# Layer 0's input projection moved up beside the context path, and its cross-attention keys computed inside its own attention

## What is computed

```python
def even_mixer(x, positions, w_in, sinks, sgu_ln_g, sgu_ln_b, sgu_w, sgu_b, w_out):
    h = x @ w_in                                   # 1024 -> 1792: q 512, k 128, v 128, bu 512, bv 512
    ...
    q = partial_rope(q.reshape(bsz, s_len, A_Q_HEADS, HEAD_DIM), positions)
    k = partial_rope(k.reshape(bsz, s_len, A_KV_HEADS, HEAD_DIM), positions)
    a_out = sliding_window_sink_attention(q, k, v, sinks)
    b_out = chunked_spatial_gating(jax.nn.gelu(bu), jax.nn.gelu(bv), sgu_ln_g, sgu_ln_b, sgu_w, sgu_b)
    return jnp.concatenate([a_out, b_out], axis=-1) @ w_out
...
        x = layer_norm(ALPHA * x + mix, ln1_g, ln1_b)
        x = layer_norm(ALPHA * x + memory_cross_attention(x, mem, xq, xkv, xo), ln2_g, ln2_b)
        x = layer_norm(ALPHA * x + grouped_moe(x, router_w, router_bias, e_gate, e_up, e_down), ln3_g, ln3_b)
```

## Time and profile before

| | |
|---|---|
| median of 3 runs | 2438.23 us (2437.54 to 2438.71) |
| profiled execution | 2439.04 us |
| its span | 2437.2 us |
| granted TensorE clock, mean | 0.91 of 2.4 GHz |
| PE busy | 1992.4 us, 82% |
| POOL busy | 1001.4 us, 41% |
| DVE busy, ACT busy | 737.3 us, 734.9 us, 30% each |
| HBM traffic | 479.5 MB, 197 GB/s over the span |

### The profile page before, as it was taken

One profiled execution on the slowest core, in us unless ns is written; L12 is line 12 of the kernel. 1 busy time (PEld: TensorE's weight loads), 2 busy tenths in 40 slices (PEclk: granted clock), 3 DMA queues, 4 the chain that ended last, 5 costly groups with the idle time before them and its releaser, 6 DMA issues. The chain is left out here.

```text
span 2437.2 us, 29352 instructions
## 1 busy us (share of the span) xinstructions
PE 1992.4 (82%) x11525; PEld 1507.5 (62%) x11525; DVE 737.3 (30%) x1398; ACT 734.9 (30%) x1020; POOL 1001.4 (41%) x784
## 2 busy tenths in 40 slices
PE   4569679977779869996798699985975999787998
PEld 0038469976558744443687544434844999656997
DVE  0113731132542231113232311114685111453112
ACT  0034444442323210002234010013453444343442
POOL 0048058884336300003475000007603798524885
PEclk9989789998669979998899799997997999898999
DMA  8985136653224429998444299995402466322652
GB/s 334 370 312 186 43 95 190 185 177 117 86 87 155 156 105 409 409 409 318 161 152 142 86 366 409 409 401 168 139 18 78 139 190 189 120 59 78 188 180 82
DMA packets 298162, 481.20 MB, mean 197 GB/s; under 512 B 16874, under 2 KB 200156, under 8 KB 297660
## 3 DMA queue, kind: packets, MB, share of 16 engines
q1 hardware_dynamic: 288284, 458.67, 52.9%
q10 hardware_dynamic: 9760, 20.88, 2.5%
HBM read 475.72 MB, written 3.77 MB: 197 GB/s over the span
## 5 line engine op out<-in xcount | busy, mean ns | idle before, releaser
L572 POOL TENSOR_TENSOR w_lo<-raw,w_hi 128x512 fp32r<-128x512 f32 x780 | 1001.1, 1319 | 1411.4 <-ACT w_hi L1245 1411.1
L622 PE MATMUL PS<-at_hi,w_hi 128*128 128x256 f32 x1680 | 490.1, 292 | 36.9 <-DVE at_lo L1727 32.9
L1245 ACT ACTIVATE w_hi<-raw 128x2048 fp32r<-128x2048 f32 x195 | 371.7, 1909 | 396.5 <-PE PS L624 375.3
L623 PE MATMUL PS<-at_lo,w_hi 128*128 128x256 f32 x1680 | 483.0, 287 | 0.0
L624 PE MATMUL PS<-at_hi,w_lo 128*128 128x256 f32 x1680 | 482.9, 287 | 0.0
L622 PEld LDWEIGHTS PS<-at_hi,w_hi 128*128 128x128 f32 x1680 | 330.7, 197 | 44.5 <-DVE at_lo L1727 35.3
L623 PEld LDWEIGHTS PS<-at_lo,w_hi 128*128 128x128 f32 x1680 | 330.6, 197 | 4.2 <-issue 3.1
L624 PEld LDWEIGHTS PS<-at_hi,w_lo 128*128 128x128 f32 x1680 | 330.2, 197 | 0.0
L622 PE MATMUL PS<-w_hi,at_hi 128*128 128x512 f32 (+1 forms) x480 | 192.5, 401 | 56.4 <-DVE at_lo L1727 34.6
L623 PE MATMUL PS<-w_lo,at_hi 128*128 128x512 f32 (+1 forms) x480 | 190.2, 396 | 0.0
L624 PE MATMUL PS<-w_hi,at_lo 128*128 128x512 f32 (+1 forms) x480 | 189.1, 394 | 0.0
(11 more groups left out here) (292 smaller groups left out, 2353.7 us busy)
## 6 DMA issues: line engine op xcount, KB each, us to landing
raw<-ffn_w_gu SPq DMA_DIRECT2D x132, 512.0 KB, 4.9
raw<-ada_w SPq DMA_DIRECT2D x64, 768.0 KB, 6.4
raw<-l_e_gate SPq DMA_DIRECT2D x80, 512.0 KB, 10.8
raw<-ffn_w_down SPq DMA_DIRECT2D x66, 512.0 KB, 4.2
raw<-l_e_up SPq DMA_DIRECT2D x64, 512.0 KB, 8.4
raw<-diff_w_in SPq DMA_DIRECT2D x48, 512.0 KB, 4.8
raw<-l_e_down SPq DMA_DIRECT2D x48, 512.0 KB, 13.7
H<-l_e_down SPq DMA_DIRECT2D x40, 512.0 KB, 12.7
```

The costliest lines, as they stand in the source:

```text
L572: ins = nc.gpsimd.tensor_tensor(w_lo[:, n % RING, part], raw[:, n % RAW, part], w_hi[:, n % RING, part].bitcast(F32), ALU.subtract)
L622: pe.matmul(dst, s_hi, m_hi, start=first, stop=False)
L623: pe.matmul(dst, s_hi, m_lo, start=False, stop=False)
L1245: nc.scalar.activation(w_hi[:, n % RING, :], raw[:, n % RAW, :], ACT.Copy).then_inc(hi_done, 1)
```

## The change

1. The tokens `x` are loaded early into `V[:, 0:2]` (`x_early`) and transposed into `at_hi`/`at_lo` inside the context's FFN: PE's 16 transposes stand ahead of the FFN's last down tile, ACT's and DVE's part of `to_at` beside them.
2. A second pair `at2_hi`/`at2_lo` of 16 KB a partition is added, and `RING` goes from 4 to 3, which frees 16 KB.
3. PE goes from the FFN to `gemm(2)` of `l0_w_in`. Then stand the `sgu_raw` transposes, the context's transposes (rows in `V[:, 2:4]`, into `at2`), `gemm(1)` of `l0_w_in`, the context's value tile, the last `l0_w_in` tile, and the context's key tile (`heads_t`). The weights are loaded in that order.
4. DVE computes the angles behind the context's norm, and rope right behind the context's `to_at`, ahead of the evacuation of `gemm(1)`.
5. `mem` is loaded into `V[:, 2:4]` and transposed into `at` before the attention of layer 0; the attention writes `at2`. The four `gemm_t` tiles of the keys stand inside that attention (`fill`, after items 1, 5, 9 and 13), in their own PSUM bank; ACT copies them to `KT` (no longer DVE). The attention's output gets a fixed bank.
6. In `cross(0)` the `to_at` and the `gemm_t(4)` are gone: `gemm(2)` for the values follows `w_out`. Layer 1 keeps its order.
7. `mod_cols(1)` stands inside the context's attention stage, and `rms` writes its squares to `PT`.

```diff
-RAW, RING = 4, 4
+RAW, RING = 4, 3
...
 # PE
-            def gated(n_f):
+            def gated(n_f, early=None):
...
                 for _ in range(1 + 4 * loops, steps):
                     step()
+                if early is not None:
+                    to_at(early, wait=False)
                 dn(False, True)
...
                         pv(it - 3)
+                    if fill is not None:
+                        fill(it)
...
             def cross(layer):
-                to_at(H)
-                gemm_t(4)
+                if layer == 1:
+                    to_at(H)
+                    gemm_t(4)
                 gemm(2)
...
                 if layer == 0:
+                    at_wait()
+                    gemm(2)
                     pe.wait_ge(tab_landed, 16 * 5)
-                    gemm(3)
+                    to_cols([sgu_raw[:, g, :] for g in range(8)])
+                    to_at(ctx_rows, wait=False)
+                    gemm(1)
+                    at_wait()
+                    gemm(1, 256, at=1)
                     gemm(1, 256)
-                    to_cols([sgu_raw[:, g, :] for g in range(8)])
+                    heads_t(1, 0, 1, False, at=1)
...
+                    def fill(it):
+
+                        if it % 4 == 1 and it < 16:
+                            if it > 1:
+                                pe.wait_ge(fill_freed, it // 4)
+                            gemm_t(1, own_bank=fill_bank)
+
+                    to_at(V[:, 2:4, :])
+                    attention(16, 1, scores, lambda i: i // 8 + 1, pv, fill)
...
 # ACT
                 if layer == 0:
+                    rms()
                     prm()
                     c.add("y", 4)
                     stat()
                     nc.scalar.activation(trig[:, 2:4, :, :], trig[:, 2:4, :, :], ACT.Sin).then_inc(stat_done, 1)
-                    tiles(7)
+                    tiles(4)
+                    plain(2)
+                    context_kv()
...
+                    to_at()
+                    act.wait_ge(kv_out, 64)
+
+                    def fill(it):
+
+                        if it % 4 == 2 and it < 16:
+                            c.add("tile")
+                            act.wait_ge(tile_used, c.get("tile"))
+                            j = it // 4
+                            nc.scalar.activation(KT[:, 2 * j:2 * j + 2, 0:TOK], fill_bank.rearrange("p (k t) -> p k t", k=2), ACT.Copy)\
+                                .then_inc(fill_freed, 1)
+                            ahead()
...
 # DVE
                     done()
-                    for n in range(3):
+                    for n in range(2):
                         y_to([H[:, t, n * 512:(n + 1) * 512] for t in range(NT)])
-                    y_to([H[:, t, 1536:1792] for t in range(NT)], 256, 1)
...
+                    to_at(a, b8, 1)
                     for t in range(NT):
...
                         ready(dve.tensor_copy(kd[:, :, 1, :], k2))
+                    y_to([H[:, t, 1024:1536] for t in range(NT)])
+                    context_kv()
```

More of the change, by code:

```diff
@@ L645, in to_at, with gemm @@
                     at_wait()
-            def gemm(groups, width=512):
+            def gemm(groups, width=512, at=0):
+                x_hi, x_lo = ats[at]
                 for _ in range(groups):
@@ L862, in diff @@
                 heads_t(4, 4, 0, path)
+                if not path:
+                    mod_cols(1)
                 def scores(i, m, bank):
@@ L885, in diff @@
                 to_at(H)
-                gated(F_FFN // P)
+                gated(F_FFN // P, None if path else x_early)
             diff(0)
-            mod_cols(1)
-            to_at(H)
-            gemm(1, 256)
-            heads_t(1, 0, 1, False)
-            at_wait()
             def cross(layer):
-                to_at(H)
-                gemm_t(4)
+                if layer == 1:
+                    to_at(H)
+                    gemm_t(4)
                 gemm(2)
@@ L1172, in _ @@
                 else:
+                    to_at(X)
                     gemm(2)
@@ L1193, in _ @@
                     at_wait()
-                gemm(2)
+                gemm(2, at=1 - layer)
                 cross(layer)
@@ L1637, in _ @@
                 tiles(4)
-                to_at()
+                if layer == 1:
+                    to_at()
                 norm()
-                c.add("wb", 4)
+                if layer == 1:
+                    c.add("wb", 4)
+                    tiles(4)
                 c.add("y", 2)
-                tiles(8)
+                tiles(4)
                 to_at()
@@ L2012, in gated @@
                     step()
+                if early:
+                    dve.wait_ge(x_landed, 32)
+                    for _ in range(NT):
+                        ready(dve.tensor_copy(hs[:, 0, 0:1], hs[:, 0, 0:1]))
+                    to_at()
                 c.add("tile")
@@ L2365, in _ @@
             for layer in range(2):
+                if layer == 1:
+                    to_at()
                 if layer == 0:
-                    dve.wait_ge(x_landed, 32)
-                    ready(dve.tensor_copy(hs[:, 0, 0:1], hs[:, 0, 0:1]))
-                    ready(dve.tensor_copy(hs[:, 0, 0:1], hs[:, 0, 0:1]))
-                to_at()
-                if layer == 0:
+                    a, b8 = affine_of(1, 1, 0)
+                    rms_to_h(asked=True, rows=ctx_rows)
                     D1(dve.tensor_copy(pos_f[:, :], pos_i[:, :]))
```

178 lines of the change are left out of this document (100 added, 78 removed).

## The result

The changed kernel takes 2426.07 us (median of 5 runs, 2423.81 to 2427.91) beside 2438.43 of the kernel before: ratio 0.9944, 95% interval 0.9930 to 0.9958. The forecast was 2406, with a range of 2391 to 2425; the median lies 1 us above that range. The sign was right, the gain is 12.4 us where I had 32.5. The profiled execution took 2427.91 us, with a span of 2426.1, 11.1 us less than the profiled one of before.

What follows compares the result with a forecast made beforehand. PE, busy 82% of the span, was taken as the bound through its order and pauses. The stretch shrinks from 249.5 to 214.7 us, gain 34.8, less 1.8 and 0.5, so 32.5: 2438.2 - 32.5 = 2405.7 us, range 2391 to 2425.

Steps and rivals of the forecast that it cites:

- the stretch of the table: From the end of the context's FFN to the first query tile: forecast 214.7 us, 249.5 before.
- the wait at the fourth value tile: Behind `w_out`, PE waits 0.3 us because ACT splits the fourth value tile only after the second root.
- the 2.1 us that I had for POOL at the projection's fourth tile: In `gemm(2)`, a new PE wait of 2.1 us, the fourth tile's split being late behind the angles and Sin.
- The attention: Layer 0's attention with four key tiles: 59 us, bounds 43 to 84, with the clock rising in the first tile and staying up.
- The check that I named: Attention over 70 us would show that the clock or ACT's splits were misjudged.
- Rope: Behind `gemm(1)` and the context's value tile, PE waits 3.8 us for DVE's rope, between 0 and 13.
- T: Time zero of the forecast's new order: the end of the last down tile of the context's FFN.
- The wait by that rule: Wait behind rope of 5.8 us instead of 3.8, if POOL's splits also hold up the copies at rope's end.
- The low clock behind the wait: After the rope wait, 1.7 us extra because half a tile runs at the low clock.
- Ahead of the stretch: Costs outside the 249.5 us: 1.8 us for early transposes of x, 0.5 for `mod_cols` in the context's attention.
- rival 4: Three ring slots let PE catch up with POOL in dense stages: slower, 2445 to 2460 us; chance 0.05.
- rival 2: Attention stays at the low clock, 75 to 84 us, or rope waits in full: gain 5 to 20, 2418 to 2433; chance 0.18.

Runs made afterwards that it cites:

- again: The changed kernel run and profiled once more with no edit: 2429.40 us, ratio 0.9956 to the kernel before.
- keys_before: The changed kernel with the four key tiles ahead of layer 0's attention instead of inside it: 2424.08 us, ratio 0.9937 to the kernel before.
- gate_fill: The changed kernel with two key tiles inside the attention and the other two right behind it: 2417.26 us, ratio 0.9909 to the kernel before.
- before: The kernel before the change, unedited: 2438.43 us.
- before_ring3: The kernel before with RING = 3 instead of 4 and nothing else: 2440.39 us, ratio 1.0011 to the kernel before.
- rope_late: The changed kernel with DVE evacuating `gemm(1)` ahead of rope, two further evacuations between rope's token tiles: 2413.69 us, ratio 0.9901 to the kernel before.
- combo: The changed kernel with key tiles in halves, rope's order as in `rope_late`, and rope angles with Sin in the set-up: 2407.14 us, ratio 0.9862.
- best: `combo` with two key tiles in halves within the attention and two whole ones behind it: 2396.36 us, ratio 0.9832 to the kernel before.
- pool_hold: The changed kernel with POOL's subtraction of the input projection's last tile held until rope is done: 2417.90 us, ratio 0.9902 to the kernel before.

## Why the prediction was wrong, point by point

The missing 21.4 us of the profiled execution (32.5 forecast, 11.1 found) are all accounted for: 13.6 in the stretch of the table, 5.4 ahead of it, 2.3 behind it.

- **What bounds the kernel, and the order of the new stretch: right.** Of the nine steps six came within 0.3 us, and `w_out` with the values within 1.4. Of these 1.4 us, 1.2 are the wait at the fourth value tile, 1.48 instead of 0.3: the second root came 10.0 us behind `w_out` (749.14), not 9.4, and POOL had the tile ready at 17.7, not 16.6. In one of the six luck had a part: the 2.1 us that I had for POOL at the projection's fourth tile were 1.25 in `again`, and none in the first profile, where the first tile took 1.5 us more at the low clock instead.
- **The attention: the step that failed, 59 forecast, 68.1 and 69.0 measured.** I took the clock to rise in the first key tile and to stay up between them, as it does in cross attention. It did not: 1.00 in the first fill, then 0.66 to 0.71 over the next four pieces. With it fell the second part, that the fills hide some of the items' DVE time: `keys_before` takes 66.3 us with nothing interleaved. They add waits instead: PE waits 10.3 us in this attention, 2.5 before. PE was busy 35.3 of the 37.8 us before. I used this row only for the clock. Its plain meaning was that there were 2.5 us of gaps to fill, and that what I called room was room only if the clock rose first. The sum from it would have been 37.8 + 4 x 5.8 = 61 at the least, and 7.6 us a tile were paid, (68.1 - 37.8) / 4, of which 5.6 are busy time and 1.9 waits. Why the clock falls between the tiles, no run tells. The check that I named, over 70 us, was set just above what came.
- **Rope: the second step that failed, in its size; the mechanism was right.** I had put the wait at 3.8 us; it was 7.4 and 8.5, and 9.4 in `gate_fill`. Rope began at T + 37.6, 1.7 earlier than forecast, and POOL at T + 38.7 instead of T + 41.4. I had let POOL start with the end of `gemm(1)`. With three slots the tile that POOL subtracts there may be split once PE has used the first of `gemm(1)`'s two tiles (575.22), and ACT splits it as soon as its own part of `to_at` is done, at 576.59. So eleven instructions were long, not six: 5 more at 1.0 us, less 1.7, is 3.3 of the 3.6 missing. Four of the five are copies. By the Trainium skill, "SBUF — State Buffer", two separate sides, such copies are held up as well, and the trace agrees: 1.20 us at 580.11 against 0.23 with POOL idle. The wait by that rule, 5.8 in the prediction, was nearer than mine.
- **The low clock behind the wait: right.** The last projection tile took 7.30 us, 5.8 with 1.7 on top was 7.5.
- **Ahead of the stretch: 2.3 us forecast, 7.7 measured.** From the first weight tile to the FFN's end it is 2.1 us more than before, 1.8 of them in the last three tiles, where the transposes of x stand: as forecast. The rest, 5.6 us, stood already at the first weight tile, before anything that the change touches. Over the eleven profiles that tile was used up at 165.3 to 172.9 us. The changed kernel itself had it at 172.9 and at 168.9 (`again`), so 4.0 of the 5.6 us are shown to be scatter of the execution, and kernels with the changed layout reached 165.3 and 166.8. I had no term for it; the first profile was the worst of the eleven and the slowest of its five runs.
- **Behind the stretch: 0 forecast, 2.3 measured.** It is in the second block's differential attention. Before, and after:

```profile
1761.00:1853.20 92.20, 63.15 (x316) 41.26 (x317) 72.24 (x156) 43.93 (x92) 6.79 (x5) 0.85 0.08 23
```

```profile
1747.00:1841.90 94.90, 66.30 (x320) 43.75 (x319) 72.26 (x156) 43.94 (x92) 7.08 (x6) 0.80 0.08 23
```

The instructions are the same, the granted clock is 0.80 instead of 0.85. Between two weight tiles around it the eleven kernels took either 142.6 to 143.0 us (`before`, `before_ring3`, `rope_late`, `combo`, `best`, `pool_hold`) or 145.2 to 145.3 (the other five, in which rope is as in the changed kernel). Three of the first group, `rope_late`, `combo` and `pool_hold`, lose 2.6 us in the stretch behind it instead (577.1 to 577.3 against 574.4 to 574.6). What in the placing of earlier work decides this, a thousand us later, no run tells. It stays open.
- **The ring, rival 4: right as forecast,** 3 us left in the FFN, measured 3.0 to 3.8.
- **The rivals.** What came is rival 2, in part: the attention between my 59 and its 75, rope nearer its full wait. It said 2418 to 2433 and had 0.18. Its mechanism had a row of its own (0.50 for all of the attention), while the one against it was taken from stretches of nothing but weight tiles. That comparison was the wrong one, and so was the row of cross attention: there the clock stayed at 1.00 with PE busy 17.7 of 24.0 us, here it fell with PE busier. The chance was too small.

What the experiments show of the rest of the gap: the new order of rope gives 7.8 to 10 us in this stretch, the placing of the key tiles another 7.6 to 9.8, both together with the early angles 24 to 26 (228.3 and 230.5 against 204.3). The forecast of 214.7 for this stretch is thus within reach of the change's idea, not of the places that it chose.

## What to carry to other kernels

Look at PE's own busy time before you fill an engine's "pauses": this attention, slow because PE ran at the low clock, had 2.5 us of gaps in 37.8, and a tile put in it cost more than it does alone (7.0 to 7.6 us against 5.45 to 6.15), with 1.9 us of new waits in it, while 7.6 us of true waiting behind that stage took two tiles for 3 us. When DVE work is moved, look at what frees PSUM behind it on the same engine, and at what POOL does at that time: ordering alone was worth 8 to 10 us. A forecast of some 10 us on one execution needs a term for what differs outside the changed stretch: here 4.0 us at the start between two executions of the same kernel, and 2.5 us in a later stage by its granted clock.

## What was not expected of the hardware

- Small copies on DVE (128 x 128, fp32, SBUF to SBUF) go from 0.23 to 1.20 us beside POOL's subtractions, just as the two-input ones do; all sixteen rope instructions took 4.3 us with POOL held and 15 in the changed kernel.
- PE at 93% busy (35.3 of 37.8 us) was granted half its clock throughout, fully busy from 649.4 to 659.4 us too, and in the attention with fills the clock fell again within the items behind each tile; dense pieces of half the length at half the distance held it at 1.00 for several in a row.
- The nine kernels whose program is the same up to the first weight tile (all but `combo` and `best`, which compute the angles there) had used it up 165.3 to 172.9 us into the execution; two profiles of one and the same kernel differed by 4.0 us.
